# Attention of a two-layer diffusion block: probability shares turned by query tile, scores three tiles ahead, keys and values projected before queries, weight splits ahead of the heads

## What is computed

```python
q = (rmsnorm(cq, g) @ w_uq)             # 384 -> 8 heads x (64 + 32 rotary)
kv = (rmsnorm(ckv, g) @ w_ukv)          # 256 -> 8 heads x (64 key + 64 value)
k = concat([k_nope, broadcast(rope(kpe))])
s = einsum('bqhd,bkhd->bhqk', q, k) * SM_SCALE
p = softmax(s); out = einsum('bhqk,bkhd->bqhd', p, v)
```

## Time and profile before

| | us |
|---|---|
| median of 3 runs | 1751.36 (1748.71 to 1754.73) |
| the profiled execution | 1748.31 |
| its span | 1746.5 |

### The profile page before, as it was taken

The page is one execution under the profiler, slowest core; times in us unless marked ns, Lnnn a source line. Parts: engine busy times, 40 slices in busy tenths (PEclk is TensorE's granted clock), DMA queues, the critical chain, the costliest instruction groups (busy, mean ns, idle before and its releaser), DMA issues.

```text
span 1746.5 us, 19442 instructions
## 1 busy us (share of the span) xinstructions
PE 1631.9 (93%) x7404; PEld 1269.4 (73%) x7404; DVE 1299.3 (74%) x1769; ACT 894.0 (51%) x1019; POOL 14.7 (1%) x31
## 2 busy tenths in 40 slices
PE   5998978899999999797888999999999999999996
PEld 3774446777888888685377778888787878878775
DVE  3825454688787765846447989898988989888897
ACT  3322264332222222432557776677777776777774
POOL 1000000000000000000000000000000000000000
PEclk8997999899999999898998999999999999999999
DMA  9225131354445553131026889899999999999993
GB/s 392 73 95 212 61 115 57 134 205 157 161 158 213 195 215 145 46 118 68 26 87 265 338 348 352 342 354 359 344 335 337 360 358 353 345 346 365 345 347 115
DMA packets 56004, 403.49 MB, mean 231 GB/s; under 512 B 6433, under 2 KB 6465, under 8 KB 8801
## 3 DMA queue, kind: packets, MB, share of 16 engines
q1 hardware_dynamic: 53712, 387.47, 59.1%
q0 software_dynamic: 2192, 14.70, 2.2%
HBM read 401.10 MB, written 1.05 MB: 230 GB/s over the span
## 4 chain that ended last, share of the span: by engine, by line
PE 63%; DVE 16%; ACT 5%; issue 3%; DVEq 0%; ACTq 0%
PE PS L435 18%; PE PS L437 18%; PE PS L436 18%; DVE w_lo L2234 5%; ACT w_hi L1472 3%; DVE w_lo L1595 1%; DVE arena L1608 1%; PE PS L986 1%; PE PS L728 1%; DVE small L1908 1%; PE PS L755 1%; DVE XT L1955 1%; DVE arena L1921 1%; DVE hT_lo L1743 1%; PE PS L741 1%
## 5 line engine op out<-in xcount | busy, mean ns | idle before, releaser
L2234 DVE TENSOR_TENSOR w_lo<-arena,w_hi 128x2048 fp32r<-128x2048 f32 x132 | 301.7, 2291 | 44.0 <-ACT w_hi L1472 44.0
L2234 DVE TENSOR_TENSOR w_lo<-raw,w_hi 128x2048 fp32r<-128x2048 f32 x129 | 295.0, 2291 | 32.7 <-ACT w_hi L1472 32.2
L1472 ACT CAST w_hi<-arena 128x2048 fp32r<-128x2048 f32 x132 | 251.6, 1909 | 47.3 <-PE PS L437 47.3
L1472 ACT CAST w_hi<-raw 128x2048 fp32r<-128x2048 f32 x129 | 246.9, 1916 | 44.3 <-PE PS L437 44.3
L435 PE MATMUL PS<-hT_hi,w_hi 128*128 128x512 f32 (+1 forms) x576 | 217.7, 378 | 11.3 <-DVE hT_lo L1743 9.9
L436 PE MATMUL PS<-hT_lo,w_hi 128*128 128x512 f32 (+1 forms) x576 | 214.8, 373 | 0.0
L437 PE MATMUL PS<-hT_hi,w_lo 128*128 128x512 f32 (+1 forms) x576 | 214.7, 373 | 0.0
L435 PE MATMUL PS<-w_hi,hT_hi 128*128 128x512 f32 (+1 forms) x448 | 178.3, 398 | 0.3 <-DVE w_lo L2234 0.3
L437 PE MATMUL PS<-w_hi,hT_lo 128*128 128x512 f32 (+1 forms) x448 | 174.6, 390 | 0.0
L436 PE MATMUL PS<-w_lo,hT_hi 128*128 128x512 f32 (+1 forms) x448 | 173.6, 388 | 0.0
L1595 DVE TENSOR_TENSOR w_lo<-raw,w_hi 128x2048 fp32r<-128x2048 f32 (+1 forms) x54 | 122.4, 2266 | 30.0 <-ACT w_hi L1102 29.9
(11 more groups left out here) (320 smaller groups left out, 2533.3 us busy)
## 6 DMA issues: line engine op xcount, KB each, us to landing
raw<-in_moe SPq DMA_DIRECT2D x132, 1024.0 KB, 6.4
arena<-in_moe SPq DMA_DIRECT2D x132, 1024.0 KB, 6.6
raw<-in_ffn SPq DMA_DIRECT2D x33, 1024.0 KB, 4.8
raw<-in_dot SPq DMA_DIRECT2D x28, 1024.0 KB, 4.9
raw<-in_ada SPq DMA_DIRECT2D x17, 1024.0 KB, 6.7
raw<-in_out SPq DMA_DIRECT2D x8, 1024.0 KB, 4.8
raw<-in_inb SPq DMA_DIRECT2D x8, 960.0 KB, 4.8
raw<-in_ina SPq DMA_DIRECT2D x5, 1024.0 KB, 5.2
```

The source lines that it names most:

```text
L1472: nc.scalar.copy(w_hi[:, x_slot(j), :], x_raw(n)).then_inc(x_hi, 1)
L2234: v.tensor_tensor(w_lo[:, x_slot(j), :], x_raw(NGR * (i % 2) + j), w_hi[:, x_slot(j), :].bitcast(F32), ALU.subtract).then_inc(x_lo, 1)
```

## The change

Part by part. (1) Turning: step u now turns the four key blocks of unit u alone, so it waits for unit u's shares only; for latent heads the copy goes to one query tile of `probT`. (2) Scores are issued up to unit u + 3, with the same three banks; before the loop three are issued, not two. (3) `ckvT` is turned before `cqT`; keys and values are projected before the queries, and values go to banks 4 to 7 in order. (4) Queries are projected by pairs of stream-heads, 2 x 256 columns into bank `pair`, and VectorE handles a pair in one operation (context) or four (latent), each 512 wide; `qtmp` and the rotary table are widened. (5) The splits of output granules 0 to 2 leave the loop: granule 0 before the key copies (ACT) and value copies (DVE), granules 1 and 2 after the key copies (ACT) and after query pairs 1 and 3 (DVE). (6) The last four `ada` granules of layer 0 are loaded after output granules 0 to 2.

```diff
         plan += [("ina", l, i) for i in range(1, 3)]
         plan += [("inb", l, i) for i in range(4)]
         if l == 0:
-            plan += [("ada", 0, i) for i in range(2 * BEFORE, 20)]
-        plan += [("out", l, i) for i in range(4)]
+            plan += [("ada", 0, i) for i in range(2 * BEFORE, 16)]
+        plan += [("out", l, i) for i in range(3)]
+        if l == 0:
+            plan += [("ada", 0, i) for i in range(16, 20)]
+        plan.append(("out", l, 3))
         if l == 0:
             before = dots_ahead()
...
         V = A(4096, NT, 512)
-        qtmp = A(6144, 256)
+        qtmp = A(6144, 512)
...
-        out_splits = {0: (4, 9, 12), 1: (1, 3, 5)}
...
                     plain(6)
+                for k in range(KKV):
+                    o = bank(f"ckvT {l} {k}")
+                    for t in range(NT):
+                        eng.wait_ge(dve_done, after(f"ckvn {l} {t}"))
+                        i = nc.tensor.transpose(o[:, P * t:P * t + P], Bm[:, t, 640 + P * k:640 + P * k + P], ident[:, :])
+                    i.then_inc(pe_done, 1)
+                    did(f"ckvT {l} {k}")
...
-                        eng.wait_ge(dve_done, after(f"ckvn {l} {t}"))
-                        i = nc.tensor.transpose(o[:, P * t:P * t + P], Bm[:, t, 640 + P * k:640 + P * k + P], ident[:, :])
-                    i.then_inc(pe_done, 1)
-                    did(f"ckvT {l} {k}")
...
-                for k in range(KQ):
-                    eng.wait_ge(act_done, after(f"cqTs {l} {k}"))
                 eng.wait_ge(*loaded[f"mla {l}"])
-                for h in range(HEADS):
-                    o = bank(f"q {l} {h}")
-                    for k in range(KQ):
-                        i = mm(o[:, sp], wuq[:, k, h, :], cqT[:, k, sp], start=k == 0, stop=k == KQ - 1)
-                    i.then_inc(pe_done, 1)
-                    did(f"q {l} {h}")
                 for k in range(KKV):
                     eng.wait_ge(act_done, after(f"ckvTs {l} {k}"))
                 for pr in range(4):
...
                 for t in range(NT):
-                    o = bank(f"v {l} {t}", (6, 7, 5, 4)[t])
+                    o = bank(f"v {l} {t}", 4 + t)
                     for k in range(KKV):
                         i = mm(o, ckvT[:, k, P * t:P * t + P], wukv[:, k, 512:1024], start=k == 0, stop=k == KKV - 1)
                     i.then_inc(pe_done, 1)
                     did(f"v {l} {t}")
+                for k in range(KQ):
+                    eng.wait_ge(act_done, after(f"cqTs {l} {k}"))
+                heads = attention_plan(streams)[0]
+                for pair in range(len(heads) // 2):
+                    o = bank(f"q {l} {pair}", pair)
+                    for j in range(2):
+                        s, h = heads[2 * pair + j]
+                        for k in range(KQ):
+                            i = mm(o[:, 256 * j:256 * j + 256], wuq[:, k, h, :], cqT[:, k, 256 * s:256 * s + 256],
+                                   start=k == 0, stop=k == KQ - 1)
+                    i.then_inc(pe_done, 1)
+                    did(f"q {l} {pair}")
                 if l == 0:
...
-                    eng.wait_ge(dve_done, after(f"qTs {l} {h}"))
+                    eng.wait_ge(dve_done, after(f"qTs {l} {n // 2}"))
...
                     for t in ((2 + j,) if s else (0, 1)):
                         q = slice(0, 512) if s else slice(256 * t, 256 * t + 256)
-                        i = mm(o[:, q], qT[0:96, h, P * t:P * t + P], KT[0:96, h, 0:512 if s else 256], start=True, stop=True)
+                        a = 256 * (n % 2) + P * (t % 2)
+                        i = mm(o[:, q], qT[0:96, n // 2, a:a + P], KT[0:96, h, 0:512 if s else 256], start=True, stop=True)
...
-                def turn_p(n, half):
+                def turn_p(u):
+                    n, j = units[u]
                     s, h = heads[n]
-                    u = first[n] + half
+                    eng.wait_ge(dve_done, after(f"ps {l} {u}"))
                     o = bank(f"pT {l} {u}", 3 + u % 3)
-                    for t in range(2):
-                        own = first[n] + t if s else u
-                        eng.wait_ge(dve_done, after(f"ps {l} {own}"))
-                        for b in range(2):
-                            at = P * (2 * half + b) if s else 256 * t + P * b
-                            i = nc.tensor.transpose(o[:, 256 * b + P * t:256 * b + P * t + P],
-                                                    prob[:, own % 4, at:at + P], ident[:, :])
+                    for b in range(4):
+                        at = P * b if s else 256 * (b // 2) + P * (b % 2)
+                        to = P * b if s else 256 * (b % 2) + P * (b // 2)
+                        i = nc.tensor.transpose(o[:, to:to + P], prob[:, u % 4, at:at + P], ident[:, :])
                     i.then_inc(pe_done, 1)
                     did(f"pT {l} {u}")
...
-                ahead_to(2)
+                ahead_to(3)
...
-                        ahead_to(first[n] + half + 3)
-                        turn_p(n, half)
+                        ahead_to(first[n] + half + 4)
+                        turn_p(first[n] + half)
                     if n and n % 2 == 0:
                         pv(n // 2 - 1)
                 pv(len(heads) // 2 - 1)
...
                     save_row(0, 6)
+                for k in range(KKV):
+                    eng.wait_ge(pe_done, after(f"ckvT {l} {k}"))
+                    o = bank_of(f"ckvT {l} {k}")
+                    a = PAR["kvg"][0] + k
+                    act(ckvT[:, k, :], o, ACT.Copy, scale=par[:, l, a:a + 1]).then_inc(act_done, 1)
+                    did(f"ckvTs {l} {k}", f"read ckvT {l} {k}")
...
@@ -1302,12 +1307,14 @@
                     did(f"KTpe {l}", f"read kpT {l}")
                 if l == 0:
                     save_row(0, 7)
+                upto(gindex[("out", l, 0, 0)])
                 for pr in range(4):
                     eng.wait_ge(pe_done, after(f"k {l} {pr}"))
                     o = bank_of(f"k {l} {pr}")
                     for j in range(2):
                         nc.scalar.copy(KT[0:64, 2 * pr + j, :], o[64 * j:64 * j + 64, :]).then_inc(act_done, 1)
                         did(f"KTs {l}", f"read k {l} {pr}")
+                upto(gindex[("out", l, 2, 0)])
                 if l == 0:
                     save_row(0, 8)
...
                     if u >= 4:
-                        m = units[u - 4][0]
-                        eng.wait_ge(pe_done, after(f"pT {l} {first[m] + heads[m][0]}"))
+                        eng.wait_ge(pe_done, after(f"pT {l} {u - 4}"))
...
-                def save_turned(n, half):
-                    u = first[n] + half
+                def save_turned(u):
+                    n, j = units[u]
                     eng.wait_ge(pe_done, after(f"pT {l} {u}"))
                     if n >= 4:
                         eng.wait_ge(pe_done, after(f"pv {l} {(n - 4) // 2}"))
-                    nc.scalar.copy(probT[:, n % 4, 2 * half:2 * half + 2, :],
-                                   bank_of(f"pT {l} {u}").rearrange("p (b q) -> p b q", q=256)).then_inc(act_done, 1)
+                    q = P if heads[n][0] else 256
+                    to = probT[:, n % 4, :, P * j:P * j + P] if heads[n][0] else probT[:, n % 4, 0:2, :]
+                    nc.scalar.copy(to, bank_of(f"pT {l} {u}").rearrange("p (b q) -> p b q", q=q)).then_inc(act_done, 1)
                     did(f"pTs {l} {u}", f"read pT {l} {u}")
...
-                        save_turned(n, half)
+                        save_turned(first[n] + half)
...
-                    if n in out_splits[l]:
-                        upto(gindex[("out", l, out_splits[l].index(n), 0)])
...
                 g = gindex[("out", l, 0, 0)]
                 root_table()
-                upto(g + 2)
+                upto(ahead(g, 2))
                 for k in range(KD):
                     if k >= 2 and k % 2 == 0:
-                        upto(g + 2 + k // 2)
+                        upto(ahead(g, 2 + k // 2))
...
-                for h in range(HEADS):
-                    eng.wait_ge(pe_done, after(f"q {l} {h}"))
-                    o = bank_of(f"q {l} {h}")
-                    if 0 in streams:
-                        v.tensor_scalar(qT[0:96, h, 0:256], o[0:96, 0:256], SM_SCALE, None, ALU.mult).then_inc(dve_done, 1)
-                        did()
...
-                    v.tensor_scalar(qT[0:64, h, q], o[0:64, q], SM_SCALE, None, ALU.mult).then_inc(dve_done, 1)
-                    did()
-                    v.tensor_tensor(qT[64:96, h, q], o[64:96, q], ropeq[64:96, 0:256], ALU.mult).then_inc(dve_done, 1)
-                    did()
-                    v.tensor_tensor(qtmp[64:96, :], o[96:128, q], ropeq[96:128, 256:512], ALU.mult).then_inc(dve_done, 1)
-                    eng.wait_ge(dve_done, did(f"read q {l} {h}"))
-                    v.tensor_tensor(qT[64:96, h, q], qT[64:96, h, q], qtmp[64:96, :], ALU.add).then_inc(dve_done, 1)
```

(39 more changed lines are left out.)

1 line of the change is left out of this document (removed).

## The result

The changed kernel takes **1720.22 us** (median of 4 runs, 1718.34 to 1721.74), the kernel before 1751.71 (median of 4 in the same session): a ratio of 0.9821, with a 95% interval of 0.9803 to 0.9839. The forecast of 1722 is 2 us off, and no rival came true. The profiled execution of the changed kernel took 1721.74 us, with a span of 1719.9. It is the slowest of its four, and the one before was the fastest of its own. So the two traces differ by 26.6 us and the medians by 31.5.

The account below looks back on a forecast made before the run. TensorE, busy 93% of the span, was taken as the bound. Gains of 20.7 us (layer 0) and 10.7 (layer 1) less 2 of handovers made 29, from 1748.3 to 1719, or 1722 against the median; range 1713 to 1736.

Parts of the forecast that it names:

- Layer 0's lead-in: Up to layer 0's first transposition: projections start 1.4 us late, so that transposition comes at 223.6, against the old 222.21.
- the possible 2.5: Layer 0's query projections: twice as many weight loads, at worst 2.5 us more; the forecast took none.
- Layer 0's loop: Layer 0's attention from the first transposition: 39.5 us of TensorE work plus 0.6 bare copy, 20.7 us gained.
- handovers: Both attention loops: uncovered handovers between engines cost 0.05 us a unit, 2 us over 40 units.
- Layer 1: Layer 1's projections and attention: TensorE stands 8.5 us before the fourth score; end 879.0 against 889.69, 10.7 us gained.
- a slow clock afterwards: Layer 1, after the 8.5 us stand: 2.5 us lost to the lower clock, ends 1.8 and 3.6.
- Passed on whole: After attention: the output projection starts with the same granules ready, everything behind is chained, so the whole gain is kept.
- The fourth rival: Behind each attention a load or split is late and most gain goes: about 10 us gained, 1741; chance 0.06.
- Units at 2.1 us: First rival, attention loops: scores wait for banks ScalarE has not read, 2.1 us a unit instead of 1.8; 1734, chance 0.2.
- A slow clock through the loops: Second rival: TensorE falls to 1.2 GHz inside both attention loops and stays there; 36 us slower, 1788, chance 0.04.
- The sum: Whole kernel: 20.7 + 10.7 - 2 = 29.4 us gained, rounded to 29.
- The wait that goes: Attention loops: TensorE's 0.8 us idle before a head's second tile, released by VectorE's scaling, goes with what follows from it.

Follow-up runs that it names:

- e_scores_two: The changed kernel with scores issued two units ahead instead of three (part 2 undone): 1727.96 us, ratio 0.9865 to the kernel before.

## Why the prediction was right, and where it was not

**Layer 0's lead-in.** Said: the keys wait 1.4 us for the rotary key copies, then keys, values and queries cost what they cost before. Measured: 1.79; keys to first transposition 43.66 us, against 43.3 forecast. The queries with twice the weight loads took 20.88 us for the 20.87 of the earlier trace rows, so taking none of the possible 2.5 was right. Everything upstream stands 2 us later in this trace, in code that the change does not touch, within the 158.2 to 162.6 us that the thirteen traces span, which is one part of why the traces differ by less than the medians.

**Layer 0's loop.** Said: 39.5 us of work and 0.6 bare, 40.1, beside 2 us of handovers over both layers. Measured: 42.18, so the handovers cost 2.1 here alone.

**Layer 1.** Said: third and fourth score late by 8.5 us, a pair at 2.9, a slow clock afterwards for 2.5, and 29 from the fourth score to the output product. Measured: 0.91 + 7.70 = 8.6, 2.88, 5.25 us at clock 0.50, which is 2.6 lost, and 863.51 - 833.44 = 30.1.

**Passed on whole.** From layer 0's output product to layer 1's first latent transposition the traces take 523.0 and 523.6 us, and behind layer 1's output product 856.4 and 856.8. The fourth rival is out.

**The other rivals.** Units at 2.1 us: out, no pause stands before the scores. A slow clock through the loops: out, layer 0's loop ran at 1.00, layer 1's at 0.94 with the slow part at its start. The Trainium skill's rule on this (TensorE: Matmul & The Clock Gate, section "A second HAM failure mode: psum-queue depth-cycling") is told there of a kernel in bf16. The traces of this one, in fp32, do not bear it out.

**The sum.** From a matmul ahead of all that the change touches (161.03 us, 159.07 before) to layer 0's output product the traces take 106.8 and 125.4 us: 18.6 gained, where 20.7 less 1 was said. In layer 1, from the first latent transposition (790.85, 808.04) to the output product, they take 72.7 and 81.7: 9.0, where 10.7 less 1 was said. With the 1.0 of the two stretches above it is 28.6, and less the 2.0 lost upstream 26.6, the difference of the traces. Each layer is short of the forecast by about 1 us, which the loops show as handovers. The gain of 29 lies between the 26.6 of the traces and the 31.5 of the medians, so that the median came within 2 us is in part luck; what bears the forecast out is the sum by stretches.

**The step that was wrong** is the reason, not the size: "The wait that goes is the 0.8 us before a head's second tile and what follows from it." It names one cause for the idle time. There are two, and the earlier trace rows held the second: of the 12.5 us in 14 waits the longest is 3.5, no pause of 0.8. Timeline of VectorE, then TensorE, in the kernel before:

```profile
234.78 2.29 DVE L1595 TENSOR_TENSOR w_lo<-raw,w_hi 128x2048 fp32r<-128x2048 f32 x1 [2.70 <-ACT w_hi L1102]
```

```profile
238.54 1.09 PE L741 MATMUL PS<-ident,arena 128*128 128x128 f32 x4 [3.47 <-DVE arena L1921]
```

A split inside the loop stands ahead of that wait. The early splits, which the prediction only placed beside the projections and charged with 4.4 us in layer 1, are worth 15.1 us net. Depth and turning together are worth 25.4 us with the splits early and 20.8 with them in the loop. With the splits out of the loop each of these two edits does most of the other's work, so turning by unit, which the prediction put first, adds nothing to deeper scores that the loops show (42.5 and 28.2 us without it, 42.2 and 28.2 with it). With the splits in the loop it still takes 4.0 us off layer 1's, and nothing off layer 0's (51.2 without it, 52.1 with it). The sum came out right since it was taken from TensorE's own work, which does not ask which edit lets it run.

## What to carry to other kernels

Write down, for an engine that runs a loop in order, how long its own order gives each round trip through the other engines (here 2.16, 3.46 or 4.76 us) and how long the trip takes (here 4.0, the other units' work on the same queues counted). Slack that falls short of the trip at every step costs at every step (3.46 us here, 5.7 us in layer 0's loop). Where it fell short at every second step only, the loops lost nothing. Then look for single long operations on the helpers' queues. One that is longer than the slack costs TensorE a pause, and here the pauses of 2.30 and 3.13 us cost its clock as well. Spread it over the loop, or move it to where its engine waits.

## What the runs showed that was not expected

Pauses of 2.30 and 3.13 us were each followed by a granted clock of about 0.50 for some 6 us, while three pauses of 0.52 to 0.71 us within 5 us were not: the same VectorE work of 2.9 us, in one piece or in four, gave clock 0.52 or 1.00. Nor were the pauses of 0.8 us a head in the kernel before, or the single pauses of 1.79 and 1.91 us before the changed kernel's keys, behind which its clock stayed at 1.00.

A trace that lists 3.6 us of idle time can hide more: e_scores_two lost 5.7 us in layer 0's loop against the changed kernel, and 2.3 of it is listed as idle. The starts show it all: each latent unit's slips by some 0.2 us.
